# One stage of a fused network on one core: the second of two interleaved matrix inversions moved up to one level behind the first, and the two halves of heads solved side by side

## What is computed

```python
def step(S, inp):
    r_t, w_t, k_t, v_t, kk_t, a_t = inp
    sa = jnp.einsum('bhij,bhj->bhi', S, kk_t)
    S = (S * w_t[:, :, None, :]
         - sa[..., None] * (kk_t * a_t)[:, :, None, :]
         + v_t[..., None] * k_t[:, :, None, :])
    return S, jnp.einsum('bhij,bhj->bhi', S, r_t)
```

## Time and profile before

| | us |
|---|---|
| median of three runs | 1991.85 (1991.8 to 1993.58) |
| profiled execution | 1992.51 |
| its span | 1990.7 |
| mean granted clock of TensorE, share of full | 0.993 |

### The profile page before, as it was taken

The page is one execution under the profiler, slowest core; times in us unless marked ns, Lnnn a source line. Parts: engine busy times, 40 slices in busy tenths (PEclk is TensorE's granted clock), DMA queues, the critical chain, the costliest instruction groups (busy, mean ns, idle before and its releaser), DMA issues.

```text
span 1990.7 us, 33822 instructions
## 1 busy us (share of the span) xinstructions
PE 1932.9 (97%) x12748; PEld 1694.6 (85%) x12748; DVE 1524.3 (77%) x2144; ACT 1149.5 (58%) x1714; POOL 371.7 (19%) x179
## 2 busy tenths in 40 slices
PE   7999998999999999999999899999999999999997
PEld 6888997888888889988879789888988788888885
DVE  6777886777777778677767766777786888988886
ACT  5444565544554455654455645444566777777775
POOL 2222031222232210222222222222003000000000
PEclk9999999999999999999999989999999999999998
DMA  9555442665555554355544105655562788888894
GB/s 354 192 190 190 150 147 68 205 192 189 172 190 190 190 182 155 130 189 190 190 153 170 50 34 190 194 190 191 187 223 77 286 330 326 315 326 325 325 333 180
DMA packets 73403, 401.08 MB, mean 201 GB/s; under 512 B 8256, under 2 KB 8384, under 8 KB 41152
## 3 DMA queue, kind: packets, MB, share of 16 engines
q1 hardware_dynamic: 72848, 397.81, 57.7%
q10 hardware_dynamic: 432, 1.57, 0.2%
HBM read 398.30 MB, written 1.05 MB: 201 GB/s over the span
## 4 chain that ended last, share of the span: by engine, by line
PE 84%; DVE 9%; PEld 3%; ACT 2%; issue 1%; DMA 0%; SPq 0%; ACTq 0%; DVEq 0%; PEldq 0%
PE psum L821 20%; PE psum L343 13%; PE psum L344 13%; PE psum L345 13%; PE psum L801 11%; PE psum L576 2%; PE psum L588 2%; DVE w_lo L311 2%; PE psum L1186 2%; PE psum L3703 1%; PE psum L578 1%; DVE w_lo L317 1%; PEld psum L345 1%; PEld psum L343 1%; PEld psum L344 1%
## 5 line engine op out<-in xcount | busy, mean ns | idle before, releaser
L311 DVE TENSOR_TENSOR w_lo<-ring,w_hi 128x1024 fp32r<-128x1024 f32 x498 | 741.6, 1518 | 172.9 <-ACT w_hi L304 171.7
L304 ACT ACTIVATE w_hi<-ring 128x1024 fp32r<-128x1024 f32 x744 | 740.0, 1051 | 204.6 <-PEq L537 104.6
L317 POOL TENSOR_TENSOR w_lo<-ring,w_hi 128x1024 fp32r<-128x1024 f32 x132 | 325.6, 2467 | 1091.8 <-ACT w_hi L304 1091.8
L821 PE MATMUL psum<-fT,w_hi 128*128 128x512 f32 x1760 | 421.4, 391 | 3.8 <-ACT w_hi L304 3.8
L821 PEld LDWEIGHTS psum<-fT,w_hi 128*128 128x128 f32 x1760 | 329.9, 188 | 71.9 <-ACT w_hi L304 4.2
L343 PE MATMUL psum<-w_hi,hT_hi 128*128 128x512 f32 (+3 forms) x656 | 241.5, 368 | 5.5 <-DVE O L1732 2.3
L343 PE MATMUL psum<-w_hi,act_hi 128*128 128x512 f32 x596 | 234.2, 393 | 0.9 <-DVE act_lo L3983 0.9
L801 PEld LDWEIGHTS psum<-fT,w_lo 128*128 128x128 f32 x1760 | 226.0, 191 | 8.9
L344 PE MATMUL psum<-w_lo,act_hi 128*128 128x512 f32 x596 | 233.4, 392 | 0.0
L345 PE MATMUL psum<-w_hi,act_lo 128*128 128x512 f32 x596 | 232.1, 390 | 0.0
L345 PE MATMUL psum<-w_hi,hT_lo 128*128 128x512 f32 (+3 forms) x656 | 231.8, 353 | 0.0
(11 more groups left out here) (582 smaller groups left out, 2518.1 us busy)
## 6 DMA issues: line engine op xcount, KB each, us to landing
ring<-in_stream SPq DMA_DIRECT2D x249, 1024.0 KB, 5.5
ring<-in_stream SPq DMA_DIRECT2D x248, 512.0 KB, 4.2
tables<-in_tables SPq DMA_DIRECT2D x1, 2005.0 KB, 19.4
gain_row<-in_gains ACTq DMA_DIRECT2D x3, 512.0 KB, 3.7
rows<-in_rows SPq DMA_DIRECT2D x1, 1288.0 KB, 22.2
X<-in_x SPq DMA_DIRECT2D x1, 1024.0 KB, 5.0
result<-X SPq DMA_DIRECT2D x2, 512.0 KB, 3.2
columns<-in_columns SPq DMA_DIRECT2D x1, 993.0 KB, 15.1
```

Source lines behind the costliest of these rows:

```text
L304: act.activation(part(w_hi, g, i), ring[:, k, i * PART:(i + 1) * PART], ACT.Copy) \
L311: dve.tensor_tensor(part(w_lo, g, i), ring[:, k, i * PART:(i + 1) * PART], part(w_hi, g, i).bitcast(F32), ALU.subtract) \
L317: pool.tensor_tensor(part(w_lo, g, 2), ring[:, k, 2 * PART:STEP], part(w_hi, g, 2).bitcast(F32), ALU.subtract) \
L821: pe.matmul(psum[:, 4 + 2 * (s % 2) + o, :], w[0][:, o, k, :], fT[:, k, :, :].rearrange("p a c -> p (a c)"), start=k == 0, stop=False, ski ...
```

## The change

Three things. First, r_rhs, r_sa and r_s1 get a second copy each (r_rhs_too, r_sa_too, r_s1_too), so the halves no longer take turns with them. Second, stream b runs one level behind stream a instead of two or more, in the order of PE, ACT, DVE and POOL alike. Third, what follows the inversions is reordered: `right_side(1, 0)` and `solved(1, 0)` go up beside those of half 0, both second chunks come after both first ones, `turn(0, 4)` goes before `turn(1, 0)`, and the numbers of `keep_warm` fall from 1 and 6 to 0 and 2. No computation is added or left out.

```diff
-                    take("r_unused_too", [P, STEP - 8 * P - 1024 - 512 - 256])
+                    r_rhs_too = take("r_rhs_too", [P, 4, 64])
...
+            r_sa_too, r_s1_too = take("r_sa_too", [P, 4, 64]), take("r_s1_too", [P, 2, P])
+
+        r_rhs, r_sa, r_s1 = (r_rhs, r_rhs_too), (r_sa, r_sa_too), (r_s1, r_s1_too)
...
             right_side(0, 0)
-            update_products(pe, a, 6)
-            level_products(pe, b, 4)
+            update_products(pe, b, 5)
+            right_side(1, 0)
+            level_products(pe, b, 6)
             solved(0, 0)
-            update_products(pe, b, 4)
+            update_products(pe, b, 6)
+            gating(0, range(4))
             state(0)
-            level_products(pe, b, 5)
+            solved(1, 0)
             result(0, 0)
-            update_products(pe, b, 5)
             right_side(0, 1)
-            gating(0, range(4))
-            level_products(pe, b, 6)
-            solved(0, 1)
-            update_products(pe, b, 6)
-            result(0, 1)
-            right_side(1, 0)
-            skip_banks(5)
             gating(1, range(4))
-            solved(1, 0)
             state(1)
             result(1, 0)
+            solved(0, 1)
             right_side(1, 1)
+            result(0, 1)
+            solved(1, 1)
             turn(0, 0)
-            solved(1, 1, 1)
-            turn(1, 0)
             result(1, 1)
             turn(0, 4)
-
-            out_tensor(pe, "rwkv", at, after_first=lambda: turn(1, 4), turns=1, warm=6)
+            turn(1, 0)
+
+            out_tensor(pe, "rwkv", at, after_first=lambda: turn(1, 4), turns=1, warm=2)
...
             def turns():
-                for t, q in ((0, 0), (1, 0), (0, 4)):
-                    turn(t, q)
+                turn(0, 0)
+                root(1, 0)
+                turn(0, 4)
+                turn(1, 0)
+                root(1, 1)
                 split_hi(act, g + 1, g + 1, (0,), freed="rwkv y 0 1")
-                root(1, 1)
+                turn(1, 4)
                 split_hi(act, g + 1, g + 1, (1, 2), freed="rwkv y 0 1")
-                turn(1, 4)
...
             update_vector(dve, a, 2)
             masked(0, "R")
             decayed(1)
+            update_vector(dve, b, 1)
             update_vector(dve, a, 3)
             masked(0, "B")
             group_mean()
-            update_vector(dve, b, 1)
+            update_vector(dve, b, 2)
             update_vector(dve, a, 4)
```

More of the change, by code:

```diff
@@ L2873, in from_state @@
                 if c == 1:
-                    pe.matmul(b[:, ti * P:(ti + 1) * P], x[:, x0 + 2 * half + ti, P:SEQ], r_s1[:, ti, :], start=True, stop=False)
+                    pe.matmul(b[:, ti * P:(ti + 1) * P], x[:, x0 + 2 * half + ti, P:SEQ], r_s1[half][:, ti, :], start=True, stop=False)
             def right_side(half, c):
@@ L2893, in solved @@
                 for ti, par, hh, m, v in heads(half, c):
-                    ins = pe.matmul(b[:, hh * 64:hh * 64 + 64], r_U[half][:, m, :], r_rhs[:, hh, :], start=True, stop=True)
+                    ins = pe.matmul(b[:, hh * 64:hh * 64 + 64], r_U[half][:, m, :], r_rhs[half][:, hh, :], start=True, stop=True)
                 ins.then_inc(*rwkv.tensor(f"rwkv sa {half} {c}"))
@@ L2916, in state @@
                     pe.matmul(b[:, ti * P:(ti + 1) * P], r_kt[:, tile], r_v[:, 0, tile], start=True, stop=False)
-                    ins = pe.matmul(b[:, ti * P:(ti + 1) * P], r_bt[:, tile], r_sa[:, 2 * ti:2 * ti + 2, :], start=False, stop=True)
+                    ins = pe.matmul(b[:, ti * P:(ti + 1) * P], r_bt[:, tile], r_sa[half][:, 2 * ti:2 * ti + 2, :], start=False, stop=True)
                 ins.then_inc(*rwkv.tensor(f"rwkv ds {half}"))
@@ L3360, in state @@
                 for ti in range(2):
-                    does(f"rwkv s1 {half} {ti}", dve.scalar_tensor_tensor, r_s1[:, ti, :], bank(f"rwkv ds {half}")[:, ti * P:(ti + 1) * P],
+                    does(f"rwkv s1 {half} {ti}", dve.scalar_tensor_tensor, r_s1[half][:, ti, :], bank(f"rwkv ds {half}")[:, ti * P:(ti + 1) * P],
                          r_f[:, 2 * half + ti:2 * half + ti + 1], table("pair_ones"), ALU.mult, ALU.mult)
@@ L3396, in rwkv_vector @@
             group_mean()
-            update_vector(dve, b, 1)
+            update_vector(dve, b, 2)
             update_vector(dve, a, 4)
+            update_vector(dve, b, 3)
             masked(1, "L")
-            update_vector(dve, b, 2)
             update_vector(dve, a, 5)
             masked(1, "R")
+            update_vector(dve, b, 4)
             group_scale()
-            update_vector(dve, b, 3)
             masked(1, "B")
             update_vector(dve, a, 6)
-            update_vector(dve, b, 4)
+            update_vector(dve, b, 5)
+            update_vector(dve, b, 6)
+            gating(0)
             state(0)
-            update_vector(dve, b, 5)
             result(0, 0)
             variances(0, 0)
-            update_vector(dve, b, 6)
-            gating(0)
-            result(0, 1)
-            variances(1, 0)
-            normalise(0, 0)
+            state(1)
             gating(1)
-            state(1)
-            normalise(1, 0)
             result(1, 0)
@@ L3422, in rwkv_vector @@
             g = first_step[at] + len(R_KINDS)
+            normalise(0, 0)
             split_lo(dve, g, g, (0,))
             normalise(0, 1)
+            result(0, 1)
+            variances(1, 0)
             split_lo(dve, g, g, (1,))
-            split_lo_last(dve, g, g)
             turn(0, 0)
-            turn(1, 0)
-            turn(0, 4)
             result(1, 1)
             variances(1, 1)
+            turn(0, 4)
+            normalise(1, 0)
+            split_lo_last(dve, g, g)
+            turn(1, 0)
+            normalise(1, 1)
             split_lo(dve, g + 1, g + 1, (0,))
-            normalise(1, 1)
             split_lo(dve, g + 1, g + 1, (1,))
```

81 lines of the change are left out of this document (42 added, 39 removed).

## The result

The changed kernel took 1999.12 us in the median of 10 runs (1995.36 to 2003.46); the kernel before, in 10 runs on the same chips, 1993.01 (1991.11 to 1998.07). The ratio is 1.0029, with a 95% interval from 1.0020 to 1.0038: slower, and above my range, which ended at 1996.5. The profiled execution took 1997.13 us.

A forecast was written before the change was run, and what follows sets the result against it. PE and the chain of levels bound the stage through the inversions, with instruction blocks pacing PE, then DVE. The 8.3 us gained shrank to -0.3: 1991.6 from the median, +0.8 for low clock, forecast 1992.3; range 1987.3 to 1996.5.

The forecast's parts named there:

- DVE's stretch: From result(1, 0) at 1172.1 to the last turn: 22.2 us of DVE work left, ending at 1194.3 before ACT's wait.
- the sum: Whole stage: first weight step ends at 1197.3 instead of 1197.6, so -0.3 us.
- The rival that came true: Clock falls at level 2 of b, in the chunks or at the end: 1994.5 to 1997 us, chance 0.25.
- The low clock in the inversions: From about 1133: +1 to +2 us while instruction blocks set the pace; after 1141 or in chunks, up to half its length.
- Blocks of instructions: PE waits for instructions every 125 matmuls, about 4.1 us; rival that they don't hold PE: 1987.8 to 1990, chance 0.2.
- the very 1160.7: Time at which the last inversion leaves PE, against 1169.0 in the old order.
- the wait at level 2 of b: In the inversions, PE waits until about 1132.9 for b's level 1 update on DVE, behind decayed(1).
- 11.2 us from the last inversion to the end of `result(1, 0)`: Chunk products on PE behind the inversions: 11.4 us together, with no wait.
- the buffers free: Second copies of buffers add no instruction, let half 1's first copies not wait for half 0, and cost nothing.
- the wait of DVE for ACT at the end: Before the low part of turn(1, 4), DVE waits about 0.8 us for ACT's high part.
- The 8.3 us: Inversions leave PE 8.3 us sooner, but this was idle time on DVE; rival of full gain: 1984, chance 0.05.

The follow-up runs named there:

- warmed: Changed kernel with 9 unread keep_warm matmuls ahead of result(0, 1) on PE; 2.6 us over the kernel before.
- copies: Changed kernel with the ACT copies solved(0, 1) and right_side(1, 1) ahead of root(0, 1); 3.6 us over the kernel before, ratio 1.0012.
- lastdve: Changed kernel with turn(1, 4) on DVE right behind normalise(1, 1), ahead of three low weight parts; stage end +78.31 us.
- before_third: Third profile of the unedited kernel before; stage end +74.16 us.
- packed_decay: Changed kernel: two ACT copies ahead of root(0, 1), ACT's turn(1, 4) last, DVE idle time filled, b's level 1 update ahead of decayed(1); 0.9983 of kernel before.
- decay: Changed kernel with only level 1's update of stream b ahead of decayed(1) on DVE; last inversion out at +37.35 us, stage end no sooner.
- inv_decay: Changed kernel with the old order behind the inversions, and b's level 1 update ahead of decayed(1) on DVE; stage end +72.72 us.
- before_decay: Kernel before with level 3's update of stream a ahead of decayed(1) on DVE; 0.1 us under the kernel before, stage end +72.07.
- fed: packed_decay with products behind the inversions reordered by what DVE gets to do from them; stage end +77.32 us.
- after: The changed kernel itself, first profile, against the kernel before; 1999.12 us, ratio 1.0029, stage end +80.29.
- before_again: Second profile of the unedited kernel before; stage end +76.8 us, last inversion out at +48.25.
- inv_only: Changed kernel with the old order behind the inversions, keeping new buffers and inversion order; 0.3 us over the kernel before, stage end +75.25.
- copies_again: Second execution of copies, with no further edit; 1.7 us over the kernel before, stage end +78.10.
- before: The kernel before, without the change, first profile; 1993.01 us, stage end +76.83.
- halves: Changed kernel with half 0's products first again behind the inversions on PE, ACT and DVE; stage ended 1.1 us behind copies.

## Why the prediction was wrong

**The step that failed** is the one on the second half: "`result(1, 0)` is there at 1172.1. *DVE's stretch.* (...) there remain 22.2: DVE would end at 1194.3". Wrong was to let the stretch run from there as if PE would keep ahead of DVE. I followed PE only up to `result(1, 0)`. Behind it the new order had put `root(0, 1)` ahead of the copy of `solved(0, 1)` on ACT, and I didn't lay the two next to each other. That wait alone would have cost nothing, as warmed shows. It cost 2.2 us through the clock, and the low clock at the end, of which I had only spoken as a rival, 1.3.

**With the clock up the sum comes out, partly by luck.** It had the end of the stage at 1197.3 - 1120.77 = +76.5, and copies measured +76.56. But DVE's stretch began 1.2 us sooner than forecast (+50.1 for +51.3) and was 1.2 us longer: 24.2 for the 22.2 and 0.8 of wait. The 22.2 held short gaps, about 0.9 us in all; the same 41 instructions were busy 21.3 us before, 21.9 in copies and 22.1 after, and the wait for ACT was 1.26.

**The rival that came true** had the right mechanism at the wrong places. I looked for the low clock at the gap of level 2 and at the end, and it came there as well (3.4 us at 1134.4, 3.4 at 1199.2, of which the second cost 1.3). The third, which decided, stood behind a wait that was not in my sum. I had written that it "decides from 8 us of low clock on after 1157"; it was 10.2 us, and the kernel lost. My price for 10.2 us was up to 5.1. The runs show 2.2: DVE had earlier results and weight parts to work on, and was busy 7.78 of those 10.2 us. The Trainium skill, TensorE: Matmul & The Clock Gate, section on HAM oscillation, reckons half of the throttled time as the penalty, which would be the same 5.1; this case's 2.2 is less than half of that.

**The low clock in the inversions** I had called cheap where blocks of instructions set the pace, and put at up to half of its length after 1141. At level 2 it was cheap: lastdve is the one run with the wait of 3.14 us and no low clock behind it, and its last inversion is out no sooner (+38.96, against +38.89 after). Further on, before matrix B of half 1, before_third shows about 2 us for 6.8. So part of what the change took away was worth something, and the 3.46 us by which the stage grew are a sum: copies, which has the new order with one short low clock, stands level with the kernel before and its long one (76.56, 76.83); to that come 2.4 up to DVE's last turn and 1.3 behind it. Against before_third, whose low clock is as short, copies is 2.4 us longer (74.16).

**Blocks of instructions.** Waits put down to issue every 4 us, as I forecast them, are hardly to be seen after: one of 1.04 us. PE's other waits, of 3.14, 1.67 and 0.89 us (for ACT, at 1143.67), lie where they would have been. Take the first away, as in packed_decay and decay, and they come back; so they do in lastdve, where the low clock behind it is away (0.93, 1.47, 0.66 and 0.71 us). But in decay and packed_decay the inversions were 1.6 and 2.9 us faster with them, so the blocks were not the only pace; that rival too was half right. That the last inversion came out at the very 1160.7 was partly luck, since the stage began 1.0 us later: 9.4 us were gained, not 8.3.

**Right:** the wait at level 2 of b behind `decayed(1)` (to 1134.14, forecast 1132.9, in a stage that began 1.0 later); 11.2 us from the last inversion to the end of `result(1, 0)`, forecast 11.4; the buffers free; the wait of DVE for ACT at the end, forecast 0.8, measured 1.26.

**The 8.3 us.** They were never worth much. inv_decay and before_decay are the cleanest pair, neither with a low clock and both with the old order behind the inversions: new order of the inversions +72.72, old order +72.07. The last inversion is out at +36.8 and +43.6, but the first result of half 0 reaches DVE at +39.6 and +39.1. Running the inversions one level apart brings the second half sooner and the first no sooner, and DVE starts with the first.

**Open.** The times differ by 6.1 and 7.3 us, the stages by 3.5 and 3.9; what the rest of the time is, no run shows. In the other direction before_decay's stage is 4.8 and 2.4 us shorter and its time 0.1 and 0.6. Span less stage is between 1913.9 (the first profile of the kernel before) and 1920.7 (fed), 1913.9 to 1920.3 over the six executions with the old order, and it goes with the low clock outside the stage, of which the two first profiles of the kernel before have 18 us and before_decay has 36.5. Those low clocks come with either order: one at -86 in after and in before_again, one at +419 in before_third and in inv_only. One or two profiles of a kernel can't tell whether the kernels differ there; that they don't is likelier by these numbers, but not shown. Nor does any run put back the numbers of `keep_warm` alone, so whether the four matmuls fewer ahead of the first weight step have a part in the low clock at the end is open.

## What to carry to other kernels

Where PE waits 2 us or more, price what the clock does behind the wait, not only the wait: here the clock fell at 18 of 23 such waits. Where the wait is cheap to keep, matmuls that nobody reads can fill it; nine of them took the price away here. When an order is rewritten on one engine, lay each copy that the next group of matmuls waits for beside what stands ahead of it on its own engine, up to the end of the stage and not only to the milestone that one expects to bind. And a part that is ready 8 us sooner is worth nothing if the consumer starts with another part: look at when its first input comes.

The best kernel of the study is packed_decay, 0.9983 (0.9971 to 0.9996) and 0.9992 (0.9983 to 1.0001) of the kernel before in two tries.

## What I had not expected of the hardware

The length of a wait doesn't tell whether the granted clock falls. Over all profiles it fell during the wait or within 2.3 us behind it at 8 of 9 waits of 3.13 to 3.14 us, at 5 of 7 of 2.55, at none of 2 of 2.42 (copies and copies_again), at 4 of 4 of 2.23 to 2.25, at the one of 2.01, and at 5 of 6 of 1.61 in the thin work of the earlier trace rows, but at none of 7 of 1.66 to 1.67, which stand at level 3 of b. Nor does it tell for how long: at the same wait for ACT the low clock was 10.2 us long in the two executions of the changed kernel and 13.7 in lastdve and decay, and at the wait before matrix B of half 1 it was 10.2 us in three executions of the old order and 3.4 in before_third. So the length of such a stage differs from execution to execution of one kernel: before had +76.83 and, once, +74.16, before_decay +72.07 and +74.41, copies +76.56 and +78.10. A difference of that size between two single profiles, as in halves, doesn't show a cause by itself; the main reading rests on DVE's stretch, which was 26.4 and 26.7 us with that low clock and 24.2 in each of the three executions without it.
